# Two-layer retention and RG-LRU decoder step: the order of VectorE and ScalarE in the retention heads, and the PSUM banks of a layer's first k tiles

## The chip, the cores and the metric

One core of one Trainium2 chip runs one program that is launched once. The metric is device time in microseconds from start to end of that program. The kernel before has a median of 2622.69 us over 3 runs.

## The reference

A prompt of 512 tokens and 8 samples of one token each pass through two layers that share their weights. Cut to the part around the change:

```
h = RMSNorm(x)
q, k, v, g_ret, x_lru, y_lru, g_a, g_b = split(h @ w_in)
q = rope(q), k = rope(k) * 256**-0.5          # 4 heads of 256; v has 512 a head
o, S_new = retention(q, k, v, S0)             # S0 = 0 (prompt) or state_ret (samples)
o = groupnorm(o) * gn_gain
ret_branch  = (silu(g_ret) * o) @ w_ret_out
lru_branch  = (gelu(y_lru) * rg_lru(conv(x_lru))) @ w_lru_out
x = x + (sig(g_a) * ret_branch + sig(g_b) * lru_branch) @ w_o
x = x + SwiGLU(RMSNorm(x)); after the last layer a final RMSNorm
```

Retention multiplies a decayed score matrix of q and k with v, adds q times the state of each sample, and updates each sample's state of 256 x 512 numbers (0.5 MB). Everything is float32. The kernel gets that precision from TensorE by splitting each operand into a high part of reduced precision and the low remainder, and by adding three products: high·high, low·high and high·low.

## The kernel before

**Tiles.** The 520 tokens lie along the free axis in two halves of 260; channels lie on the 128 partitions. An output tile of a projection is 128 channels x 520 tokens in two PSUM banks. `whole` computes one from 8 k blocks: 48 matmuls of 128x260. Each layer runs four heads (`one_head`, head 0 written out with `first=True`, heads 1 to 3 in a loop), then the LRU branch, the merge, w_o and the FFN.

**Weights.** They come as a stream of units (1024 columns). SyncE loads a unit, GpSimd (POOL) splits it (L334 high, L337 low in two parts), TensorE (PE) uses it. There are two buffers each, and POOL may start unit u+1 when PE starts unit u.

**A head on PE.** Two q tiles, in heads 1 to 3 the transposes of the last head's output (`turned_back`), two k tiles, in heads 1 to 3 the 8 tiles m0 to m7 of the output projection of the head before (`ret_out`, k dimension 4 blocks, so 24 matmuls each), four v tiles, scores, transposes, gate tile 0, transposes of v (`v_by_token`), gate tiles 1 to 3, then the attention products (`attend`, L576) and the new states (`final_state`, L584). `read_out(b)`, L513, multiplies q by the state of sample b. There are eight of them, placed between and inside the tiles. Each needs the state's high and low part, of which one copy exists. So read-out b, ScalarE's high part of b+1 (`state_high`, L1313) and VectorE's low part of b+1 (`state_low`, L877) follow one another.

**PSUM slots.** q, k, ret_out, v and gate tiles of the heads take turns in two slots `PP`: tile n waits until VectorE has read tile n-2 (`tile_begin`, semaphore t_free, counted in order of the reads). Four further banks `AUX` hold scores, transposes, attention and read-outs. Outside the heads they are half of a ring of four tile slots.

**VectorE (DVE), ScalarE (ACT) and POOL** each run one queue in written order. On DVE `rotate` reads a pair of tiles and forms the rotary result: L845 and L846 read the even tile, L849 and L850 the odd one, L853 and L854 combine them. `read_back` (L765) multiplies the last head's output with the gate and `og_split` (L774) makes its low part, which ret_out m0 waits for. `ret_add` (L780) adds a ret_out tile to `ret_acc`. `gate` (L948) reads a gate tile, `v_low` (L933) and L941 make low parts of v and of the scores, `new_state` (L957) updates a sample's state. ScalarE stores a state after new_state and loads the next one into its place, in the order of its queue.

**A layer's start.** The first two q tiles are made while the norm is still being summed (`twin`). The sums go to AUX banks 0 and 1 (L424), ScalarE takes the root, DVE the reciprocal (L729), scales the cosine and sine tables and then reads the q tiles.

The order inside a head on DVE, before:

```
rotate(0, QF, lambda: None, lambda: None if first else read_back(hh - 1))
...
rotate(KT, KF, new_gain, lambda: None)      # new_gain: og_split(hh), then the new gain
q_parts()                                   # low part of q, q pairs for the read-outs
```

## Time and profile before

| | us |
|---|---|
| median of 3 runs (lowest, highest) | 2622.69 (2619.82, 2623.14) |
| the profiled execution, whole | 2620.91 |
| its span | 2619.1 |
| layer 0: start to end of head 3 | about 0 to 543 |
| layer 0: LRU to FFN | about 543 to 1322 |
| layer 1: heads | about 1322 to 1837 |

A line of the timeline gives start and duration in us, the engine, the source line, the operation with what it writes and reads, and how often it stands there in a row. In brackets stand the idle time of the engine before it and what ended that. Matmuls overlap, so two of them in a row start about 0.24 us after the two before, though each pair shows 0.40. The mean granted TensorE clock of the run is 0.988 of full speed.

### The profile page before, as it was taken

How to read it: one execution, taken by the hardware profiler on the slowest of the kernel's cores; microseconds unless marked ns; L12 is line 12 of the kernel's file. 1: busy time of each engine (PE TensorE's matmuls, PEld its weight loads, DVE VectorE, ACT ScalarE, POOL GpSimd, SP SyncE). 2: the span in 40 equal slices, each digit the busy share in tenths (PEclk: the TensorE clock that was granted, in tenths of full speed). 3: DMA queues.
4: the chain of work that ended last, by engine and by line, in shares of the span. 5: the costliest groups of instructions: out<-in, count | busy, mean ns of one | idle time of the engine just before them, and what ended most of it. 6: DMA issues, size and time to landing. Idle time of an engine off the chain costs nothing.

```text
span 2619.1 us, 52416 instructions
## 1 busy us (share of the span) xinstructions
PE 2495.5 (95%) x19636; PEld 2402.5 (92%) x19636; DVE 1364.9 (52%) x1715; ACT 722.6 (28%) x1109; POOL 1550.7 (59%) x1265
## 2 busy tenths in 40 slices
PE   6999999999999999999989999999999999999997
PEld 6888888899999999999988888888999999999997
DVE  7765656568754542122357656665686546321223
ACT  3423232336731111001123141414367211100111
POOL 4354545457676666666643635353677766666664
PEclk9999999999999999999999999999999999999998
DMA  5545454432233322322246363535222322223222
GB/s 171 186 148 178 149 169 160 158 121 93 75 95 91 97 91 84 94 89 89 89 152 221 106 221 113 204 124 186 85 88 80 98 90 92 89 89 96 88 82 88
DMA packets 121748, 315.69 MB, mean 121 GB/s; under 512 B 12192, under 2 KB 12960, under 8 KB 121568
## 3 DMA queue, kind: packets, MB, share of 16 engines
q1 hardware_dynamic: 60480, 199.78, 24.1%
q10 hardware_dynamic: 61088, 113.34, 12.6%
q8 instruction: 134, 2.20, 0.4%
q14 instruction: 46, 0.38, 0.0%
HBM read 272.69 MB, written 40.38 MB: 120 GB/s over the span
## 4 chain that ended last, share of the span: by engine, by line
PE 68%; DVE 14%; DVEq 6%; issue 4%; ACT 3%; DMA 2%; ACTq 1%; POOL 1%; POOLq 1%; SPq 0%
PE proj L350 40%; PE aux L350 21%; DVE split_scratch L877 2%; PE aux L513 2%; DVE scratch L1044 2%; DVE scratch L957 2%; DMA scratch<-in_sret 1%; DVEq L1189 1%; PE aux L535 1%; PE aux L584 1%; DVE split_scratch L774 1%; POOL w_low L337 1%; POOLq L335 1%; DVE split_scratch L941 1%; PE aux L576 1%
## 5 line engine op out<-in xcount | busy, mean ns | idle before, releaser
L337 POOL TENSOR_TENSOR w_low<-w_raw,w_high 128x512 fp32r<-128x512 f32 (+2 forms) x840 | 1120.3, 1354 | 62.8 <-issue 3.1
L334 POOL TENSOR_SCALAR w_high<-w_raw 128x1024 fp32r<-128x1024 f32 (+3 forms) x420 | 430.0, 1024 | 981.6 <-PE proj L350 770.3
L350 PE MATMUL proj<-x_high,w_high 128*128 128x260 f32 x2816 | 579.8, 287 | 69.1 <-DVE scratch L948 25.2
L350 PE MATMUL proj<-x_low,w_high 128*128 128x260 f32 x2816 | 572.2, 285 | 0.0
L350 PE MATMUL proj<-x_high,w_low 128*128 128x260 f32 x2816 | 572.2, 285 | 0.0
L350 PEld LDWEIGHTS proj<-x_high,w_high 128*128 128x128 f32 x2816 | 442.3, 191 | 83.8 <-DVE scratch L948 27.3
L350 PEld LDWEIGHTS proj<-x_low,w_high 128*128 128x128 f32 x2816 | 439.9, 191 | 0.0
L350 PEld LDWEIGHTS proj<-x_high,w_low 128*128 128x128 f32 x2816 | 439.6, 191 | 0.0
L350 PE MATMUL proj<-split_scratch,w_high 128*128 128x260 f32 x2544 | 414.3, 285 | 16.6 <-DVE ret_acc L780 11.9
L350 PEld LDWEIGHTS proj<-split_scratch,w_high 128*128 128x128 f32 x2544 | 351.7, 189 | 24.3 <-DVE ret_acc L780 13.6
L350 PE MATMUL aux<-x_high,w_high 128*128 128x260 f32 x1280 | 259.1, 283 | 3.2 <-POOL w_low L337 1.7
L350 PE MATMUL aux<-x_high,w_low 128*128 128x260 f32 x1280 | 257.7, 283 | 0.0
L350 PE MATMUL proj<-split_scratch,w_low 128*128 128x260 f32 x1272 | 257.4, 284 | 0.0
L350 PE MATMUL aux<-x_low,w_high 128*128 128x260 f32 x1280 | 257.3, 283 | 0.0
L350 PE MATMUL aux<-split_scratch,w_high 128*128 128x260 f32 x1456 | 235.5, 284 | 0.1
L350 PEld LDWEIGHTS aux<-x_high,w_high 128*128 128x128 f32 x1280 | 197.3, 188 | 5.4 <-POOL w_low L337 3.3
L350 PEld LDWEIGHTS aux<-split_scratch,w_high 128*128 128x128 f32 x1456 | 199.4, 188 | 1.8 <-POOL w_low L337 0.3
L350 PEld LDWEIGHTS proj<-split_scratch,w_low 128*128 128x128 f32 x1272 | 197.5, 190 | 0.0
L350 PEld LDWEIGHTS aux<-x_high,w_low 128*128 128x128 f32 x1280 | 197.2, 188 | 0.0
L350 PEld LDWEIGHTS aux<-x_low,w_high 128*128 128x128 f32 x1280 | 196.8, 188 | 0.0
L877 DVE TENSOR_TENSOR split_scratch<-scratch,split_scratch 128x512 fp32r<-128x512 f32 x128 | 135.3, 1096 | 78.1 <-ACT split_scratch L1313 78.1
L1313 ACT ACTIVATE split_scratch<-scratch 128x512 fp32r<-128x512 f32 x128 | 76.1, 626 | 271.2 <-PE aux L513 271.2
(181 smaller groups left out, 2665.9 us busy)
## 6 DMA issues: line engine op xcount, KB each, us to landing
w_raw<-in_wstream SPq DMA_DIRECT2D x252, 512.0 KB, 3.6
scratch<-in_sret ACTq DMA_DIRECT2D x96, 512.0 KB, 6.4
out_ret_s<-scratch ACTq DMA_DIRECT2D x64, 512.0 KB, 3.5
w_raw<-in_wstream SPq DMA_DIRECT2D x72, 448.0 KB, 3.2
w_raw<-in_wstream SPq DMA_DIRECT2D x48, 384.0 KB, 3.0
scratch<-v_rows ACTq DMA_DIRECT2D x64, 256.0 KB, 4.0
w_raw<-in_wstream SPq DMA_DIRECT2D x48, 320.0 KB, 2.8
out_ret_p<-scratch ACTq DMA_DIRECT2D x8, 512.0 KB, 3.2
```

The lines of the kernel that those rows point to most:

```text
L334: pool.tensor_scalar(WH[:, j, w], WR[:, j, w], 1.0, 0.0, ALU.mult, ALU.add)
L335: pool.drain()
L337: m = pool.tensor_tensor(WL[:, j, part], WR[:, j, part], WH[:, j, part].bitcast(F32), ALU.subtract)
L350: m = pe.matmul(out, wt[:, w, blk * P:(blk + 1) * P], x[xi], start=first and n == 0, stop=last and n == 2)
L513: m = pe.matmul(aux("RO", 2 * NS), QP[:, d, b, :], part[:, d, :], start=b == d == n == 0, stop=b == NS - 1 and d == KT - 1 and n == 1)
L535: m = pe.matmul(aux(f"SC{j}")[:, 0:SEQ - j * P], a[:, d, j * P:(j + 1) * P], b[:, d, j * P:SEQ], start=d == n == 0, stop=d == KT - 1 and n ...
L576: m = pe.matmul(aux(f"AT{t}"), a[:, w], b[:, j, :], start=j == n == 0, stop=j == t and n == 2)
L584: m = pe.matmul(aux(f"ST{d}"), a[:, j, d * P:(d + 1) * P], b[:, j, :], start=j == n == 0, stop=j == TT - 1 and n == 2)
L877: tt(SSL[:, d, :], SS[b % SRING][:, d, :], SSH[:, d, :].bitcast(F32), ALU.subtract).then_inc(s["s_low"], 1)
L957: stt(SS[r], SS[r], KDC[:, TT:TT + 1], TS[u % 2], ALU.mult, ALU.add).then_inc(s["s_new"], 1)
L1044: m = stt(XCF[:, t, d:SEQ], xr[:, 0:SEQ - d], CUR[:, PC_CW + c * CW + j:PC_CW + c * CW + j + 1], XCF[:, t, d:SEQ], ALU.mult, ALU.add)
L1313: A(SSH[:, d, :], SS[b % SRING][:, d, :], copy).then_inc(s["s_high"], 1)
```

## The change

**A layer's first k tiles.** In head 0 they are written to AUX banks: tile 2 to banks 2 and 3, tile 3 to banks 0 and 1, not to the two slots. They wait for the weights alone, tile 3 also for the root of the norm (x_sd), since the norm's sums lie in its banks. The first two v tiles then wait for the reads of q tile 0 and 1, the first read-out for the read of k tile 2.

PE, the end of `twin` in head 0. Before, with the wait for a free slot (t_free):

```order
L350 MATMUL proj<-x_high,w_low 128x260 x2
L367 REGISTER_ALU
L358 REGISTER_ALU [waits w_split]
L350 MATMUL proj<-x_high,w_high 128x260 [waits t_free]
L350 MATMUL proj<-x_high,w_high 128x260
L350 MATMUL proj<-x_low,w_high 128x260 x2
```

Now (proj is the pair of slots, aux the four banks):

```order
L359 MATMUL proj<-x_high,w_low 128x260 x2
L376 REGISTER_ALU
L359 MATMUL aux<-x_high,w_high 128x260 [waits w_split]
L359 MATMUL aux<-x_high,w_high 128x260
L359 MATMUL aux<-x_low,w_high 128x260 x2
L359 MATMUL aux<-x_high,w_low 128x260 x2
```

Between the first k tile and the second one, now:

```order
L359 MATMUL aux<-x_low,w_high 128x260 x2
L359 MATMUL aux<-x_high,w_low 128x260 x2
L516 REGISTER_ALU
L376 REGISTER_ALU [waits x_sd]
L359 MATMUL aux<-x_high,w_high 128x260 [waits w_split]
L359 MATMUL aux<-x_high,w_high 128x260
```

The first k tile goes to aux and t_free is gone from it. The second one waits for x_sd.

**Order of DVE in heads 1 to 3.** q's odd tile, read_back, the combination of q, og_split, and only then the even k tile. After it come q's parts, the gain, state_low(0) and then the odd k tile. ret_add(0) stands between the two combinations of k. The read-outs on PE stand behind m1, m3, m5, m7 and behind each v tile, no longer behind m2, m4, m6 and in the middle of v tiles. ScalarE makes the high part of state 0 ahead of k's.

DVE, heads 1 to 3, from og_split's last two on. Before (p_done: the tile is made, og_high: ScalarE's high part; the even k tile has been read ahead of these rows):

```order
L774 SCALAR_TENSOR_TENSOR split_scratch<-scratch,gn_cur,split_scratch 128x520 [waits og_high] x2
L862 ISA
L862 COPY gn_cur<-params_cur 128x4
L718 REGISTER_ALU
L849 TENSOR_TENSOR scratch<-proj,sin_r 128x520 [waits p_done]
L850 TENSOR_TENSOR scratch<-proj,cos_r 128x520
L853 TENSOR_TENSOR scratch<-scratch 128x520
```

Now (the lines moved by some 20):

```order
L791 SCALAR_TENSOR_TENSOR split_scratch<-scratch,gn_cur,split_scratch 128x520 [waits og_high] x2
L932 ISA
L735 REGISTER_ALU [waits sfin_st]
L866 TENSOR_TENSOR scratch<-proj,cos_r 128x520 [waits p_done]
L867 TENSOR_TENSOR scratch<-proj,sin_r 128x520
L855 ISA
L856 SCALAR_TENSOR_TENSOR split_scratch<-scratch,split_scratch 128x1040 [waits qk_high]
L888 COPY q_pairs<-split_scratch 128x2x8 x2
L935 ISA
L935 COPY gn_cur<-params_cur 128x4
L895 REGISTER_ALU
L896 TENSOR_TENSOR split_scratch<-scratch,split_scratch 128x512 [waits s_high]
```

The split stood between the reads of the two k tiles and stands now ahead of both. Between them stand now L856 (low part of q), L888, L935 and L896 (state_low), and the odd tile's read, L872, follows these.

**Gate 0.** Low parts of the scores come first, then the read of gate tile 0, then all four v_low. ScalarE makes the scores' high parts and issues the loads of the v rows ahead of all four high parts of v.

DVE behind the scores, heads 1 to 3. Before:

```order
L933 TENSOR_TENSOR split_scratch<-aux,split_scratch 128x512 [waits kv_high]
L718 REGISTER_ALU
L948 TENSOR_TENSOR scratch<-proj,rinv 128x520 [waits p_done]
L956 ISA
L957 SCALAR_TENSOR_TENSOR scratch<-scratch,kd_cur 128x1024 [waits t_mul]
```

Now (L987 is the gate's read, L975 v_low):

```order
L982 TENSOR_TENSOR split_scratch<-scratch,split_scratch 128x128 [waits st_high]
L735 REGISTER_ALU
L987 TENSOR_TENSOR scratch<-proj,rinv 128x520 [waits p_done]
L974 REGISTER_ALU
L975 TENSOR_TENSOR split_scratch<-aux,split_scratch 128x512 [waits kv_high]
```

The gate's read stands ahead of the four v_low, no longer behind them.

The diff, cut to its core:

```diff
         def pp(idx):
             return PP[:, slot(idx), :, 0:HALF]
 
+        def key_banks(idx):
+
+            b = 2 * (QK - 1 - idx)
+            return AUX[:, b:b + 2, 0:HALF]
+
+        def first_keys(idx):
+
+            return [key_banks(idx)[:, c, :] for c in range(2)]
...
 
-            def whole(ub, u, tb, idx, hi, lo, midway=None):
+            def whole(ub, u, tb, idx, hi, lo, midway=None, into=None, freed_by=None):
 
 
 
                 unit_begin(ub, u)
-                tile_begin(tb, idx)
-                outs = [PP[:, slot(idx), c, 0:HALF] for c in range(2)]
+                if freed_by is not None:
+                    pe.wait_ge(s["t_free"], freed_by)
+                elif into is None:
+                    tile_begin(tb, idx)
+                outs = into or [PP[:, slot(idx), c, 0:HALF] for c in range(2)]
                 for k in range(MT):
...
                         ub, tb = ub0 - MT // 2 + head * U_HEAD, tb0 - MT + head * T_HEAD
                         uv, v0 = QK + MT // 2, QK + MT
                     if first:
-                        for r in range(RING - 1):
+                        for r in range(RING):
                             pe.wait_ge(r_free[r], layer * USES[r] + 1)
                         tile_begin(tb, 0)
                         tile_begin(tb, 1)
...
                     for i in range(KT, QK):
-                        whole(ub, i, tb, i, XH, XL)
+                        if first and i == QK - 1:
+                            pe.wait_ge(s["x_sd"], layer + 1)
+                        whole(ub, i, tb, i, XH, XL, into=first_keys(i) if first else None)
 
                     def read_out(b):
 
                         if b == 0:
+                            if first:
+                                pe.wait_ge(s["t_free"], tb + (QK - 1))
                             pe.wait_ge(s["qp_full"], hh + 1)
...
                     if first:
                         for i in range(VT):
                             whole(ub, uv + i, tb, v0 + i, XH, XL,
-                                  midway=lambda: read_out(2 * i - 1) if i else None)
+                                  midway=lambda: read_out(2 * i - 1) if i else None,
+                                  freed_by=tb + (i + 1) if i < 2 else None)
                             read_out(2 * i)
                     else:
-                        ret_out(hh, ub, QK, tb, QK, lambda m_: read_out(m_ // 2 - 1) if m_ in (2, 4, 6) else None)
+                        ret_out(hh, ub, QK, tb, QK, lambda m_: read_out(m_ // 2) if m_ % 2 else None)
                         for i in range(VT):
-                            whole(ub, uv + i, tb, v0 + i, XH, XL, midway=lambda: read_out(3 + i))
-                        read_out(NS - 1)
+                            whole(ub, uv + i, tb, v0 + i, XH, XL)
+                            read_out(MT // 2 + i)
                     pe.wait_ge(s["qk_low"], hh * 2 + 2)
 
                     for j in range(TT):
...
+                    def turned(dst, between):
+
                         dve.drain()
                         tt(dst[:, 0, :], dst[:, 0, :], RT[:, 0, :], ALU.subtract)
+                        between()
                         tt(dst[:, 1, :], dst[:, 1, :], RT[:, 1, :], ALU.add).then_inc(s["rope_done"], 1)
                         dve.drain()
...
-                    rotate(0, QF, lambda: None, lambda: None if first else read_back(hh - 1))
-                    dve.wait_ge(s["sfin_st"], hh * 16 + 16)
-                    if first:
-                        state_low(0)
-                    rotate(KT, KF, new_gain, lambda: None)
-                    q_parts()
-                    ts(KSC[:], KF[:, :, SEQ:TOK], DK ** -0.5, None, ALU.mult)
-                    if first:
+                    def key_low():
+
+                        ts(KSC[:], KF[:, :, SEQ:TOK], DK ** -0.5, None, ALU.mult)
                         low(KL, KF, KH, DK ** -0.5, 2)
-                    else:
-                        for m_ in range(MT):
-                            if m_ in (2, 4, 6):
-                                state_low(m_ // 2 - 1)
-                            ret_add(tb, QK, m_)
-                            if m_ == 0:
-                                low(KL, KF, KH, DK ** -0.5, 2)
-                    if not first:
-                        state_low(3)
-                    for e in range(VT):
-                        if e or not first:
-                            state_low(2 * e if first else e + 4)
+
+                    def value(e):
+
                         done(tb, v0 + e)
                         tt(halves(VF[:, e, :]), pp(v0 + e), halves(RINV[:]), ALU.mult
                            ).then_inc(s["t_free"], 1)
-                        if first:
+
+                    turn_even(0, QF)
+                    turn_odd(1)
+                    if first:
+                        dve.wait_ge(s["sfin_st"], hh * 16 + 16)
+                        turn_even(KT, KF)
+                        turned(QF, lambda: None)
+                        turn_odd(KT + 1)
+                        q_parts()
+                        state_low(0)
+                        turned(KF, lambda: None)
+                        dve.tensor_copy(GNC[:], CUR[:, bass.ds(head * VT + PC_GN, VT)])
+                        state_low(1)
+                        value(0)
+                        key_low()
+                        for e in range(1, VT):
+                            state_low(2 * e)
+                            value(e)
                             state_low(2 * e + 1)
+                    else:
+                        read_back(hh - 1)
+                        turned(QF, lambda: None)
+                        og_split(hh)
+                        dve.wait_ge(s["sfin_st"], hh * 16 + 16)
+                        turn_even(KT, KF)
+                        q_parts()
+                        dve.tensor_copy(GNC[:], CUR[:, bass.ds(head * VT + PC_GN, VT)])
+                        state_low(0)
+                        turn_odd(KT + 1)
+                        turned(KF, lambda: ret_add(tb, QK, 0))
+                        ret_add(tb, QK, 1)
+                        key_low()
+                        for m_ in range(2, MT):
+                            if m_ % 2 == 0:
+                                state_low(m_ // 2)
+                            ret_add(tb, QK, m_)
+                        for e in range(VT):
+                            state_low(MT // 2 + e)
+                            value(e)
...
-                    v_low(0)
                     for j in range(TT):
                         dve.wait_ge(s["st_high"], hh * TT + (j + 1))
                         w = slice(ST_OFF[j], ST_OFF[j + 1])
                         tt(STL[:, w], STF[:, w], STH[:, w].bitcast(F32), ALU.subtract
                            ).then_inc(s["st_low"], 1)
-                    for j in range(1, TT):
-                        v_low(j)
...
+                    dve.drain()
                     gate(0)
+                    for j in range(TT):
+                        v_low(j)
                     new_state(0)
...
-                    if first:
-                        state_high(0)
-                    act.wait_ge(s["rope_done"], hh * 2 + 2)
-                    A(KH, KF, copy, scale=DK ** -0.5).then_inc(s["qk_high"], 1)
                     for b in range(NS):
-                        if b or not first:
-                            state_high(b)
+                        state_high(b)
+                        if b == (1 if first else 0):
+                            act.wait_ge(s["rope_done"], hh * 2 + 2)
+                            A(KH, KF, copy, scale=DK ** -0.5).then_inc(s["qk_high"], 1)
...

```

## Rows read from the trace of the kernel before

**Rows 1.** The page, part 1: busy time, share of the span and instructions.
```profile
PE 2495.5 (95%) x19636; PEld 2402.5 (92%) x19636; DVE 1364.9 (52%) x1715; ACT 722.6 (28%) x1109; POOL 1550.7 (59%) x1265
```
**Rows 2.** Waits of PE: line waited for, us in total, times, longest us.
```profile
PE proj L350 <- DVE scratch L948: 25.2, 10, 2.6
...
PE proj L350 <- POOL w_low L337: 12.0, 17, 1.0
PE proj L350 <- DVE ret_acc L780: 11.9, 8, 1.8
PE proj L350 <- DVE scratch L846: 11.5, 2, 5.8
PE aux L513 <- DVE split_scratch L877: 10.0, 22, 0.7
...
PE aux L584 <- ACT scratch L1395: 3.7, 6, 0.8
```
**Rows 3.** Timeline of PE, layer 0, head 0: start, us, instruction, idle before.
```profile
35.64 0.80 PE L350 MATMUL proj<-x_high,w_high 128*128 128x260 f32 x2 [5.75 <-DVE scratch L846]
...
55.66 1.10 PE L513 MATMUL aux<-split_scratch,q_pairs 128*16 128x512 f32 x4 [0.93 <-DVE q_pairs L869]
...
110.06 0.51 PE L350 MATMUL proj<-x_high,w_high 128*128 128x260 f32 x2 [2.15 <-DVE scratch L948]
...
129.24 0.97 PE L584 MATMUL aux<-split_scratch 128*128 128x512 f32 x3 [0.74 <-ACT scratch L1395]
```
**Rows 4.** Chain that ended last: two output tiles (96 products) at three places.
```profile
35.64 13.34 PE proj L350 x96
...
132.95 11.55 PE proj L350 x96
...
507.01 13.22 PE proj L350 x96
```
**Rows 5.** Timeline of DVE, layer 0, head 0.
```profile
29.21 3.40 DVE L729 RECIPROCAL rinv<-rinv 128x520 f32<-128x520 f32 x1 [1.11 <-ACT rinv L1268]
...
34.89 0.69 DVE L846 TENSOR_TENSOR scratch<-proj,sin_r 128x520 f32<-128x520 f32 x1
...
109.30 0.70 DVE L948 TENSOR_TENSOR scratch<-proj,rinv 128x520 f32<-128x520 f32 x1
```
**Rows 6.** Timeline of PE, layer 0, head 1.
```profile
158.50 0.64 PE L350 MATMUL proj<-split_scratch,w_high 128*128 128x260 f32 x4
...
166.28 0.75 PE L350 MATMUL proj<-split_scratch,w_high 128*128 128x260 f32 x4 [1.80 <-DVE ret_acc L780]
...
262.39 3.01 PE L584 MATMUL aux<-split_scratch 128*128 128x512 f32 x12 [0.68 <-ACT scratch L1395]
```
**Rows 7.** Timeline of DVE, layer 0, head 1.
```profile
152.92 0.70 DVE L845 TENSOR_TENSOR scratch<-proj,cos_r 128x520 f32<-128x520 f32 x1 [2.04 <-PE proj L350]
...
154.15 4.95 DVE L774 SCALAR_TENSOR_TENSOR split_scratch<-scratch,gn_cur,split_scratch 128x520 fp32r<-128x520 f32 x4
...
159.97 0.69 DVE L849 TENSOR_TENSOR scratch<-proj,sin_r 128x520 f32<-128x520 f32 x1
...
229.17 0.69 DVE L933 TENSOR_TENSOR split_scratch<-aux,split_scratch 128x512 fp32r<-128x512 f32 x1 [3.98 <-ACT split_scratch L1348]
...
230.07 4.75 DVE L941 TENSOR_TENSOR split_scratch<-scratch,split_scratch 128x512 fp32r<-128x512 f32 x4 [0.21 <-ACT split_scratch L1353]
...
237.43 0.70 DVE L948 TENSOR_TENSOR scratch<-proj,rinv 128x520 f32<-128x520 f32 x1 [0.21 <-issue]
...
256.16 1.28 DVE L957 SCALAR_TENSOR_TENSOR scratch<-scratch,kd_cur 128x1024 f32<-128x1024 f32 x1 [2.55 <-DMA scratch<-in_sret]
```
**Rows 8.** One line each: shortest, median, longest duration in ns, first and last start.
```profile
L877 DVE TENSOR_TENSOR split_scratch<-scratch,split_scratch x128: 678/922/1779, 41.4 to 1776.0; 128x512 fp32r<-128x512 f32 x128
...
L774 DVE SCALAR_TENSOR_TENSOR split_scratch<-scratch,gn_cur,split_scratch x32: 747/1294/1790, 154.1 to 1841.9; 128x520 fp32r<-128x520 f32 x32
...
L839 DVE SCALAR_TENSOR_TENSOR split_scratch<-scratch,split_scratch x16: 1232/1239/2087, 53.0 to 1727.5; 128x1040 fp32r<-128x1040 f32 x16
```

25 lines of the change are left out of this document (10 added, 15 removed).

## The prediction

> **What bounds the kernel now.** I read the busy shares first: PE has 95% of the span, DVE 52% [rows 1]. So the time is PE's work plus its pauses, and a change that moves no matmul can only change pauses and PE's clock. The next view, the waits of PE, shows who ends them [rows 2]. Five of its lines lie in the heads (1.1 us of the second excepted): L948 (a gate tile read late by DVE) 25.2 us, L780 (ret_add) 11.9, L846 (the first q tile of a layer) 11.5, L877 (state_low) 10.0, L1395 (normalisation ahead of the second final_state) 3.7. Together 62.3 us in eight heads, 2.4% of the time. The timeline of PE gives the places, in head 0 [rows 3] and in head 1 [rows 6]. The chain gives the clock: two tiles in a row take 11.55 us at full clock but 13.34 and 13.22 directly after a long pause [rows 4], so a pause can cost up to 1.7 us beyond its own length. The timeline of DVE says how much room its queue has [rows 5, 7].
>
> **A. The first k tiles of a layer (two places).** Before, PE stops 5.75 us [rows 3] between the q tiles and the k tiles, since DVE must first form the reciprocal (from 29.21), scale two tables and read the q tile (until 35.6) [rows 5]. Now both k tiles are made in that time: from 35.64 - 5.75 = 29.9 to 29.9 + 11.55 = 41.4 [rows 3, 4]. The price is at the next stations.
> - The first v tile needs q tile 0's read, 35.6, or up to 2 us later, since POOL now splits weights beside the table products. Wanted at 41.4: hidden.
> - The first read-out, wanted one tile (half of 11.55) later at 47.2, needs q's parts and state_low(0). DVE reads q and k even by 38 to 39 (two operations a tile, 0.61 apart), combines q (two operations at 0.7 to 1.8), reads k odd at 41.6, makes q's low part (1.24 to 2.09 [rows 8]) and state_low(0) (two at 0.68 to 1.78 [rows 8]): ready at 46 to 48.5. So the 0.93 of before [rows 3] goes and 0 to 1.4 comes.
> - The second read-out needs state_low(1), now behind the combination of k: 0.5 to 2 us late. The third has k's low part ahead of it on DVE: 0 to 1.
> I take 2.3 us of new waits (range 0.5 to 4.4). Saved per layer: 5.75 + 0.93 - 2.3 = 4.4, and 1.8 for the slow stretch (13.34 - 11.55 [rows 4]): 6.2. **Two layers: 12.4.** The added wait on the fourth ring entry holds nobody: that bank pair was read before the last one of a layer, which is waited for already. The wait for x_sd is over at 29.2, long before the second k tile.
>
> **B. Gate 0 ahead of v's low parts, heads 1 to 3 (six places).** DVE stood idle 3.98 us until ScalarE had v's first high part, then ran v_low(0), 4.75 us of the scores' low parts and three more v_low, and read the gate tile at 237.43 [rows 7]; PE had waited 2.6 for it [rows 2]. Now the scores' low parts fall into that idle time, and the gate tile is read as soon as it is made. That is before 229.17, since v_low(0) reads transposes that PE made behind it: over 8 us earlier. The wait goes whole, six times 2.6 = 15.6. Behind it v_low and new_state stand earlier: 4.7 less the 1.3 by which v's high parts now stand behind the issue of four loads on ScalarE's queue, so 3.4 to 4.7. State stores and loads follow them on that queue. That matters, since the second final_state (262.39, wait 0.68 [rows 6]) hangs on a state load that lands at 256.16 [rows 7]: with PE 2.6 earlier, it must come 2.6 earlier too. I take that it does (bounds 0 and 4.7) and that 2.2 of the 3.7 us at L1395 [rows 2] go. PE then asks for gate 3 sooner than POOL can split it beside the state updates: 0.3 more at each, -1.8. Slow stretches follow this pause in some heads (13.22 against 11.55 [rows 4]); I count 4 us for six places. **15.6 + 2.2 - 1.8 + 4 = 20.0.**
>
> **B in head 0 (two places).** There two pauses stand at L948, 2.63 and 2.15 (the longest of its line [rows 2], and the second in the timeline [rows 3]). Behind gate 0 DVE runs new_state and the series of lambda, so it reads gate 1 at 109.30 [rows 5]. It is then busy without a gap, and the end of the head is its own: the second final_state at 129.24 waits for it [rows 3]. So PE's gain is what DVE's queue gains, 3.4 to 4.7, I take 4.2. **8.4.** It holds clock and waits.
>
> **C. Heads 1 to 3: og_split and the read-outs (six places).** Removed: 1.80 before m2 [rows 6], six times 10.8, and 10.0 at the read-outs [rows 2]. Read-outs now come behind whole tiles, 6.7 us apart (two ret_out tiles at a quarter of 11.55 each [rows 4], and an estimate of 0.9 for itself: four matmuls of 512 columns against the 24 of 260 in 2.9), while high part, low part and their handovers take about 4. Added: m1 must wait for k's odd tile, which DVE now reads behind og_split and state_low(0). In head 1: the combination of q ends at 152.92 - 2.04 = 150.9 [rows 7]. og_split takes 3.0 (four at 0.75, POOL at rest) to 4.95 [rows 7, 8]: 153.9 to 155.8. k even read: 155.1 to 157.0, ahead of m0 at 158.50 [rows 6], hidden. q's low part 1.24 to 2.09, pairs and gain 0.7 to 1.0, state_low(0) 1.4 to 2.7, k odd read 1.2: 159.6 to 164.0. Before it was 159.97 + 1.2 = 161.2 [rows 7], just in time for m1 at 158.50 + 2.9 = 161.4. So a new wait of 0 to 2.6; with POOL busy about half of that stretch I come to 162.1 and take 0.7. ret_add(0) is done 1.8 later, m2 wants it 3.8 later: gone. **10.8 + 10.0 - 6 x 0.7 + 1 (clock) = 17.6.**
>
> What hides the rest: low parts of k and moved ScalarE work lie beside m2 and the v tiles, with 2 us of room. No transfer changes in size or count.
>
> The Trainium skill speaks against the order in C: "SBUF — State Buffer", Who interferes with whom, says that a VectorE instruction with two SBUF inputs and a GpSimd instruction that reads SBUF exclude each other, the one that comes second waiting for the whole of the other. This trace agrees in size: L774 takes 747 ns at best, 1294 in the median, and L877 678 to 1779 [rows 8]. By the rule at full price all ten such operations between q and k odd would wait; that is rival 1.
>
> **The sum.** 12.4 + 20.0 + 8.4 + 17.6 = 58.4 us. The profiled execution took 2620.9, so 2562.5. The median of the runs shown is 1.8 above it: I predict 2564. With all new waits at zero it is 2552.
>
> **Rivals.**
> 1. *k's odd tile comes late in every head.* Two-input operations on DVE at their long values [rows 8]: read at 163.9 and m1 waits 2.5. 1.8 x 6 = 10.8 more, and the clock's 1 is lost: 2576. For it: og_split took 4.95 in before. Against it: POOL rests 1.2 to 1.5 us between units there.
> 2. *The state loads do not move.* If the transfers around 256.16 are limited by the memory and not by when they are issued, the second final_state stays where it is in six heads: 2.6 and 0.4 are lost in each, 18: 2582. For it: such loads wait 2.55 us for data [rows 7]. Against: the stores ahead of them are issued 4 us sooner, into a time in which PE had stood still.
> 3. *Slower.* The one mechanism is the chain q odd, read_back, combination, og_split, k even, q's low part, state_low, k odd. Each us by which it misses 161.4 costs six. It eats 62.6 (58.4 and the 4.2 counted for it) at 10.4 us of lateness; at 12 us the time is 2622.7 - 62.6 + 72 = 2632. By the longest durations of all (1.79, 2.09, 1.78 [rows 8]) it would be about 6 us late. So nearly excluded.
> 4. *Nothing happens*, since PE's pauses come back one by one at the next station (head 0: read-outs; heads: m1, final_state). A, B and C would have to fail together: 2620.
>
> **How the numbers follow.** Forecast (2552 to 2571) 0.62; rival 1 0.15; rival 2 0.12; both, to 2594, 0.04; better than 2552 0.04; rival 3 0.01; rival 4 0.02. The range reaches to rivals 1 and 2: 2551 to 2586, which leaves out about 0.15. A measurement of this kernel tells 0.2% (5 us) from no change. Faster by more 0.97, within it 0.02, slower 0.01.
>
> **What would show it.** In the waits of PE: L948's line nearly gone in heads 1 to 3 and one of some 0.6 us in each head 0; no pause at the q read of a layer's start, k products on aux directly behind the twin tiles, and small waits for state_low in the first two or three read-outs. A new line of 0.7 us, six times, for the read of k's odd tile (2.5: rival 1); no ret_add wait at m2. The second final_state of head 1 some 3 us nearer to its gate 0, with the state's landing the same amount nearer (if not: rival 2). Wrong would be: q's table products stretched past 41.4, or a wait of several us for w_low, POOL being locked out by DVE.

## The result, and the profile after

| | before | after |
|---|---|---|
| median of 4 runs, same chip (lowest, highest), us | 2622.07 (2619.82, 2623.14) | 2561.57 (2560.41, 2565.22) |
| profiled execution, us | 2620.91 | 2560.41 |
| its span, us | 2619.1 | 2558.6 |
| granted TensorE clock, mean | 0.988 | 0.994 |

The ratio is 0.9773, 95% interval 0.9756 to 0.979. The changed kernel is 60.5 us faster, 2.4 us below the forecast of 2564.0 and inside its range. The interval is about 4.5 us wide on either side, so the medians say nothing on those 2.4 us. The terms of the sum do: one was too high by 6.7 us, and others made up for it. That the total came so close is luck.

Part 1 of the page of after, which answers to [rows 1]. The busy time of PE fell by 17 us with the same 19636 instructions. Part of that is clock: a matmul that runs at the lower of the two levels (1.2 GHz, not 2.4) is longer, and the stretches in which the 128x260 matmuls start further apart than usual cost 22.0 us before and 11.5 after (my sum over the trace). The rest would be overlap that pauses had broken: a read-out split by a pause shows 0.63 + 0.64 us of work (at 303.21 and 304.51 before), an unbroken one 1.09.

```profile
PE 2478.6 (97%) x19636; PEld 2392.2 (93%) x19636; DVE 1342.7 (52%) x1715; ACT 720.9 (28%) x1109; POOL 1553.4 (61%) x1265
```

The waits of PE after: line waited for, us in total, times, longest us. This view answers to [rows 2].

```profile
PE proj L359 <- DVE scratch L873: 13.0, 6, 2.2
PE proj L359 <- POOL w_low L346: 10.4, 16, 1.1
...
PE aux L601 <- ACT scratch L1434: 4.8, 5, 1.4
...
PE proj L359 <- DVE scratch L987: 2.6, 2, 1.5
...
PE aux L529 <- DVE split_scratch L896: 1.3, 2, 0.6
PE aux L593 <- ACT scratch L1434: 1.1, 2, 0.6
PE proj L359 <- DVE ret_acc L797: 1.1, 2, 0.6
```

The gate's wait fell from 25.2 to 2.6 (L987, two left, both in head 0), ret_add's from 11.9 to 1.1, state_low's from 10.0 to 1.3, and the 11.5 of a layer's first q read are gone. **One line is new and large: 13.0 us for the read of k's odd tile (L873), six times 2.16.** The forecast had it at six times 0.7.

The timeline of PE after, in head 0 of layer 0 (above the three dots) and in head 1: start, us, instruction, and in brackets the idle time before it. It answers to [rows 3, 6].

```profile
47.11 1.14 PE L529 MATMUL aux<-split_scratch,q_pairs 128*16 128x512 f32 x4
...
52.24 0.63 PE L529 MATMUL aux<-split_scratch,q_pairs 128*16 128x512 f32 x2 [0.64 <-DVE split_scratch L896]
...
98.33 0.50 PE L359 MATMUL proj<-x_high,w_high 128*128 128x260 f32 x2 [1.04 <-DVE scratch L987]
...
114.45 1.65 PE L593 MATMUL aux<-split_scratch 128*128 128x512 f32 x6 [0.59 <-ACT scratch L1434]
117.54 3.02 PE L601 MATMUL aux<-split_scratch 128*128 128x512 f32 x12 [1.43 <-ACT scratch L1434]
...
152.00 0.74 PE L359 MATMUL proj<-split_scratch,w_high 128*128 128x260 f32 x4 [2.16 <-DVE scratch L873]
156.37 1.24 PE L529 MATMUL aux<-split_scratch,q_pairs 128*16 128x512 f32 x4
...
229.91 0.51 PE L359 MATMUL proj<-x_high,w_high 128*128 128x260 f32 x2 [1.10 <-POOL w_low L346]
...
246.64 2.88 PE L601 MATMUL aux<-split_scratch 128*128 128x512 f32 x12
```

In head 0 the first read-out starts at 47.11 with no wait (55.66 before), and the only wait for a state there is 0.64. In head 1, m1 starts 2.16 us late at 152.00, the read-outs have no wait, and the second final_state (246.64) has none either.

Where the time went can be read from the places at which the heads' scores begin (the first L535 before, L552 after, in us of the PE timeline):

| layer, head | 0, 0 | 0, 1 | 0, 2 | 0, 3 | 1, 0 | 1, 1 | 1, 2 | 1, 3 |
|---|---|---|---|---|---|---|---|---|
| before | 79.46 | 216.73 | 350.68 | 485.55 | 1372.91 | 1510.18 | 1644.14 | 1778.74 |
| after | 71.75 | 204.19 | 331.61 | 461.03 | 1335.73 | 1467.15 | 1594.08 | 1723.10 |
| ahead by | 7.7 | 12.5 | 19.1 | 24.5 | 37.2 | 43.0 | 50.1 | 55.6 |

Split at the last head's end and at m0 as well, the 60.5 us are: A 15.9 (7.9 and 8.0), B in head 0 7.5, B in heads 1 to 3 23.2, C 10.9, and 3 outside the heads. There two stretches at the low clock (granted clock 0.5 at 675 and at 1968 us before) are gone and one is new (at 1280 after), and the waits for w_low are 1.1 us shorter in all. Nothing in the forecast counted these 3 us.

### The profile page after: what moved, and what is told of

Same layout as the page of the kernel before. It is cut to its first block, busy times and chain, and to the rows that moved or that the text cites. A ratio compares the mean times of both kernels' runs of the same rounds, so it can differ in the third digit from the quotient of the medians.

```text
span 2558.6 us, 52418 instructions
## 1 busy us (share of the span) xinstructions
PE 2478.6 (97%) x19636; PEld 2392.2 (93%) x19636; DVE 1342.7 (52%) x1715; ACT 720.9 (28%) x1109; POOL 1553.4 (61%) x1265
## 4 chain that ended last, share of the span: by engine, by line
PE 71%; DVE 9%; DVEq 6%; issue 4%; ACT 3%; DMA 2%; ACTq 2%; POOL 1%; POOLq 1%
PE proj L359 42%; PE aux L359 23%; PE aux L529 2%; DVE scratch L1086 2%; DVEq L1231 1%; PE aux L601 1%; POOL w_low L346 1%; PE aux L552 1%; DMA scratch<-in_sret 1%; DMA scratch<-v_rows 1%; PE aux L593 1%; DVE split_scratch L896 1%; POOLq L344 1%; DVE scratch L1144 1%; ACTq L1578 1%
## 5 line engine op out<-in xcount | busy, mean ns | idle before, releaser
L346 POOL TENSOR_TENSOR w_low<-w_raw,w_high 128x512 fp32r<-128x512 f32 (+2 forms) x840 | 1110.3, 1343 | 62.9 <-issue 3.1
L343 POOL TENSOR_SCALAR w_high<-w_raw 128x1024 fp32r<-128x1024 f32 (+3 forms) x420 | 442.7, 1054 | 918.4 <-PE proj L359 695.3
L359 PE MATMUL proj<-x_high,w_high 128*128 128x260 f32 x2752 | 560.6, 285 | 32.8 <-DVE x_low L743 13.6
L359 PE MATMUL proj<-x_high,w_low 128*128 128x260 f32 x2752 | 555.4, 283 | 0.0
L359 PE MATMUL proj<-x_low,w_high 128*128 128x260 f32 x2752 | 554.9, 283 | 0.0
L359 PEld LDWEIGHTS proj<-x_high,w_high 128*128 128x128 f32 x2752 | 428.1, 189 | 45.2 <-DVE x_low L743 14.0
L359 PEld LDWEIGHTS proj<-x_high,w_low 128*128 128x128 f32 x2752 | 425.3, 189 | 0.0
L359 PEld LDWEIGHTS proj<-x_low,w_high 128*128 128x128 f32 x2752 | 424.9, 189 | 0.0
L359 PEld LDWEIGHTS proj<-split_scratch,w_high 128*128 128x128 f32 x2544 | 352.0, 190 | 25.2 <-DVE scratch L873 14.2
L359 PE MATMUL aux<-x_high,w_high 128*128 128x260 f32 x1344 | 272.0, 283 | 2.6 <-DVE residual L1223 1.4
L359 PE MATMUL aux<-x_high,w_low 128*128 128x260 f32 x1344 | 270.6, 283 | 0.0
L359 PE MATMUL aux<-x_low,w_high 128*128 128x260 f32 x1344 | 270.1, 283 | 0.0
L896 DVE TENSOR_TENSOR split_scratch<-scratch,split_scratch 128x512 fp32r<-128x512 f32 x128 | 141.5, 1146 | 24.7 <-ACT split_scratch L1355 24.7
L359 PE MATMUL aux<-split_scratch,w_low 128*128 128x260 f32 x728 | 146.3, 282 | 0.0
```

Of the source, the lines that this page charges most:

```text
L343: pool.tensor_scalar(WH[:, j, w], WR[:, j, w], 1.0, 0.0, ALU.mult, ALU.add)
L346: m = pool.tensor_tensor(WL[:, j, part], WR[:, j, part], WH[:, j, part].bitcast(F32), ALU.subtract)
L359: m = pe.matmul(out, wt[:, w, blk * P:(blk + 1) * P], x[xi], start=first and n == 0, stop=last and n == 2)
L896: tt(SSL[:, d, :], SS[b % SRING][:, d, :], SSH[:, d, :].bitcast(F32), ALU.subtract).then_inc(s["s_low"], 1)
```

## The experiments

All times are medians. Each run has the kernel before beside it on the same chip, 2620.4 to 2622.7 us. Where two changed kernels that ran on different chips are compared, the difference of their medians is good to a few us only.

### The three parts alone

**a_only** is the kernel before with the banks for the first k tiles and head 0's order on DVE up to the v tiles. **b_only** and **c_only** have the other two parts. Lines from their diffs against before, one place of each (the rest is cut):

```diff
 # a_only, PE, head 0
+                        if first and i == QK - 1:
+                            pe.wait_ge(s["x_sd"], layer + 1)
+                        whole(ub, i, tb, i, XH, XL, into=first_keys(i) if first else None)
 # b_only, DVE behind the scores
-                    v_low(0)
                     for j in range(TT):
...
+                    gate(0)
+                    for j in range(TT):
+                        v_low(j)
 # c_only, PE, heads 1 to 3
-                        ret_out(hh, ub, QK, tb, QK, lambda m_: read_out(m_ // 2 - 1) if m_ in (2, 4, 6) else None)
+                        ret_out(hh, ub, QK, tb, QK, lambda m_: read_out(m_ // 2) if m_ % 2 else None)
```

> Part A alone on the kernel before: a layer's first k tiles in four banks that are free, with the order of head 0 that goes with them; gate 0 and og_split stand as before. The trace of the changed kernel gives 7.9 and 8.0 us for A by the place at which the first scores begin. If the parts add up, PE stays that much ahead to the end of head 0 and the time is 2622 - 16 = 2606 us. The rival: VectorE has no gap at the end of head 0, so A's time stands again there as longer waits (L948 and the second final_state), and A alone gives 8 us or less: 2614 to 2618.

> Part B alone on the kernel before: the scores' low parts ahead of all of v's, gate 0 ahead of v's low parts, and v's high parts behind the issue of the state loads on ScalarE. By the landmarks of the changed kernel it gives 23.2 us in heads 1 to 3 and 7.5 in head 0: 2622 - 31 = 2591 us if the parts add up. The rival: without C, og_split comes late behind the state's last reads and the gain stands again at L780, 1 us in each head: 2597.

> Part C alone on the kernel before: og_split ahead of the first k tile, read-outs behind whole tiles. By the landmarks of the changed kernel it gives 10.9 us net: 20.8 of waits go and 6 x 2.16 us come at the second tile of ret_out. If the parts add up the time is 2622 - 11 = 2611 us and a wait of about 2.2 us for the read of the odd k tile stands in heads 1 to 3. My forecast for C, 17.6, would be 2604 with a wait of 0.7; it would be right if B, which brings PE closer to VectorE there, had made the wait longer.

| | median (lowest, highest) | ratio to before, 95% | against before | expected |
|---|---|---|---|---|
| a_only | 2601.68 (2597.98, 2603.04) | 0.9924 (0.9906 to 0.9942) | -19.9 | -16 |
| b_only | 2589.73 (2586.26, 2591.30) | 0.9878 (0.9860 to 0.9896) | -31.8 | -31 |
| c_only | 2611.76 (2609.03, 2613.17) | 0.9963 (0.9950 to 0.9976) | -9.8 | -11 |

**The parts add up** within what the medians can tell: 19.9 + 31.8 + 9.8 = 61.5, against 60.5 for the whole. The rivals by which one part eats another's gain are out. a_only keeps its lead to the end of head 0: the first final_state starts at 114.46 (122.22 before: 7.8), the second at 121.51 (129.24: 7.7). It gains 4 us more than expected behind the first heads. In its list of waits the gate's are 1.5 us shorter than before (23.7), those for w_low 1.5 and those with no releaser 1.4, and the granted clock is 0.991 against 0.988. Why part A should change these stays open.

C alone has the same new wait as in the whole. The waits of PE in c_only:

```profile
PE proj L359 <- DVE scratch L985: 25.1, 10, 2.6
...
PE proj L359 <- DVE scratch L868: 13.0, 6, 2.2
```

L868 is here the read of k's odd tile. So B, which leaves the gate's 25.1 in place here, has nothing to do with it: the wait belongs to C's own order.

### The cause of the new wait

The timeline of DVE after, head 1, ahead of the odd k tile's read, which answers to [rows 7]. L791 is og_split, L866 k's even tile, L856 q's low part, L888 the pairs, L896 state_low(0), L872 and L873 k's odd tile.

```profile
137.38 1.79 DVE L880 TENSOR_TENSOR scratch<-scratch 128x520 f32<-128x520 f32 x1
139.71 3.98 DVE L791 SCALAR_TENSOR_TENSOR split_scratch<-scratch,gn_cur,split_scratch 128x520 fp32r<-128x520 f32 x4 [0.53 <-ACT split_scratch L1330]
143.61 0.69 DVE L866 TENSOR_TENSOR scratch<-proj,cos_r 128x520 f32<-128x520 f32 x1
...
144.83 2.36 DVE L856 SCALAR_TENSOR_TENSOR split_scratch<-scratch,split_scratch 128x1040 fp32r<-128x1040 f32 x1
147.27 1.12 DVE L888 CAST q_pairs<-split_scratch 128x16 fp32r<-128x16 f32 x2
...
148.37 2.37 DVE L896 TENSOR_TENSOR split_scratch<-scratch,split_scratch 128x512 fp32r<-128x512 f32 x2
150.66 0.69 DVE L872 TENSOR_TENSOR scratch<-proj,sin_r 128x520 f32<-128x520 f32 x1
151.26 0.68 DVE L873 TENSOR_TENSOR scratch<-proj,cos_r 128x520 f32<-128x520 f32 x1
```

The timeline of POOL in the same stretch:

```profile
136.99 3.34 POOL L346 TENSOR_TENSOR w_low<-w_raw,w_high 128x512 fp32r<-128x512 f32 x2
141.72 1.42 POOL L343 TENSOR_SCALAR w_high<-w_raw 128x1024 fp32r<-128x1024 f32 x1 [1.39 <-PE proj L359]
143.29 2.79 POOL L346 TENSOR_TENSOR w_low<-w_raw,w_high 128x512 fp32r<-128x512 f32 x2 [0.15 <-issue]
147.30 1.06 POOL L343 TENSOR_SCALAR w_high<-w_raw 128x1024 fp32r<-128x1024 f32 x1 [1.22 <-PE proj L359]
148.50 3.35 POOL L346 TENSOR_TENSOR w_low<-w_raw,w_high 128x512 fp32r<-128x512 f32 x2
```

Each long operation of DVE lies beside one of POOL: q's low part and state_low(0) beside w_low (L346), the pairs beside w_high (L343). Of og_split's four operations, taken singly, the first took 1.18 us beside w_low and the last 1.53 beside w_high, and the two between them, mostly beside nothing, 0.75. The operations that read PSUM (L866, L872) keep their 0.69 beside a w_low. Two runs take this apart.

**thin_low** makes POOL's w_low short in the heads: it writes 128 columns where the kernel needs up to 512. The other columns hold old values, so its result is not the reference's and only its time is of use. w_high, all matmuls, loads and waits stay.

```diff
+            pool.memset(WL[:].rearrange("p a b -> p (a b)").bitcast(F32), 0.0)
...
+                                q = part if base else slice(part.start, part.start + P)
-                                m = pool.tensor_tensor(WL[:, j, part], WR[:, j, part],
-                                                       WH[:, j, part].bitcast(F32), ALU.subtract)
+                                m = pool.tensor_tensor(WL[:, j, q], WR[:, j, q],
+                                                       WH[:, j, q].bitcast(F32), ALU.subtract)
```

> The changed kernel, but in the 66 weight units that the heads use GpSimd writes w_low for 128 columns of each half of a unit, not for 512; the other columns hold old values, so this part of the result is not the reference's. All matmuls, loads and waits stay. It tells what stretched VectorE's operations ahead of the odd k tile: in head 1 of the changed kernel the odd k tile is read 2.16 us late, behind og_split 3.98, q's low part 2.36 and state_low(0) 2.37 us, each beside a w_low of GpSimd. My theory: those are the weight splits' doing. With them short, the three take about 2.8, 1.3 and 1.3 us (3.3 less), the wait of 2.16 goes in all six places and the time falls by 13 us or more. The rival: they take this long by themselves or beside ScalarE and the transfers; they keep their lengths within 0.5 us, and the wait of 2.16 stays.

Measured: 2534.88 us (2533.34 to 2538.82), ratio to before 0.9665, 95% interval 0.9649 to 0.9681: 26.7 below the changed kernel. The wait for the odd k tile is gone from the list of waits. The same operations on DVE, two lines further down in this kernel's code:

```profile
132.06 0.96 DVE L882 TENSOR_TENSOR scratch<-scratch 128x520 f32<-128x520 f32 x1
133.55 2.77 DVE L793 SCALAR_TENSOR_TENSOR split_scratch<-scratch,gn_cur,split_scratch 128x520 fp32r<-128x520 f32 x4 [0.53 <-ACT split_scratch L1332]
...
137.45 1.23 DVE L858 SCALAR_TENSOR_TENSOR split_scratch<-scratch,split_scratch 128x1040 fp32r<-128x1040 f32 x1
138.78 0.34 DVE L890 CAST q_pairs<-split_scratch 128x16 fp32r<-128x16 f32 x2
...
139.37 1.28 DVE L898 TENSOR_TENSOR split_scratch<-scratch,split_scratch 128x512 fp32r<-128x512 f32 x2
141.67 0.70 DVE L874 TENSOR_TENSOR scratch<-proj,sin_r 128x520 f32<-128x520 f32 x1 [1.01 <-PE proj L361]
```

og_split, q's low part and state_low(0) take 2.77, 1.23 and 1.28 us, where they took 3.98, 2.36 and 2.37: 3.4 less, and DVE now waits 1.01 for PE. **The stretching is POOL's doing.** (w_high keeps its 1.06 us in this kernel, but at 136.39 and 141.97 it lies beside reads of PSUM.) The two profiled executions differ by 24.1 us in span (2558.6 and 2534.5), and 13.0 of that are this wait. In the list of waits the gate's fall by 2.1 more, POOL's own by 2.3, those for the first norm's x_low by 2.3, those for state_low by 1.3 and ret_add's by 1.1, while the normalisation's grow by 4.2 and those with no releaser by 1.5. Of the 8 us that are left, about 5 would be the clock (0.996 against 0.994 of 2535 us, an estimate). The others I can't place.

**k_odd_first** leaves POOL alone and reads the odd k tile earlier.

```diff
                         q_parts()
+                        turn_odd(KT + 1)
                         dve.tensor_copy(GNC[:], CUR[:, bass.ds(head * VT + PC_GN, VT)])
                         state_low(0)
-                        turn_odd(KT + 1)
                         turned(KF, lambda: ret_add(tb, QK, 0))
```

> The changed kernel with one step moved in heads 1 to 3: the odd k tile is read ahead of the gain copy and of state_low(0), not behind them. My theory: the new wait of 2.16 us at the second tile of ret_out is these operations' own time on VectorE (2.4 and 0.3 us), and nothing else needs them that early: the wait goes in all six places, the first read-out (2.9 us later) still finds its state, and the time is 2561.6 - 12 = 2549 to 2552 us. The rival: state_low(0) or ret_add(0) is then late instead, a wait of 1 to 2 us stands at the first read-out or at the third tile of ret_out, and the time stays within 3 us of 2561.6.

Measured: 2547.45 us (2545.28 to 2550.57), ratio to before 0.9717, 95% interval 0.9699 to 0.9734: 14.1 below the changed kernel. The timelines of DVE and (last two rows) PE in its head 1:

```profile
148.65 0.69 DVE L872 TENSOR_TENSOR scratch<-proj,sin_r 128x520 f32<-128x520 f32 x1
149.25 0.68 DVE L873 TENSOR_TENSOR scratch<-proj,cos_r 128x520 f32<-128x520 f32 x1
149.86 0.32 DVE L936 COPY gn_cur<-params_cur 128x4 f32 x1
150.09 2.38 DVE L896 TENSOR_TENSOR split_scratch<-scratch,split_scratch 128x512 fp32r<-128x512 f32 x2
...
150.03 0.70 PE L359 MATMUL proj<-split_scratch,w_high 128*128 128x260 f32 x4
...
152.97 1.09 PE L529 MATMUL aux<-split_scratch,q_pairs 128*16 128x512 f32 x4
```

The odd tile is read by 149.9, m1 starts without a pause, and state_low(0) is done at 152.5, half a microsecond before the first read-out wants it. The pause did not come back elsewhere: the list of waits has none for the odd tile, and the others stay within 1.3 us of what they were. The 14.1 are more than the 13.0 of the pauses and than the 10 to 13 expected, but by less than these medians can tell. (The profiled execution is the slowest of the four and only 9.8 us shorter in span than that of the changed kernel. The slow stretches behind three of the pauses are gone in it, and others, at 638 and 1898 us, have come.) This kernel is faster than the one before and the changed one.

### The two halves of B

**b_scores_only** puts the scores' parts ahead of v's, on both engines, and leaves gate 0 behind v's low parts. **b_gate_only** leaves ScalarE and v_low(0) where they were and puts gate 0 ahead of the other three v_low.

```diff
 # b_scores_only against b_only
-                    dve.drain()
-                    gate(0)
                     for j in range(TT):
                         v_low(j)
+                    gate(0)
 # b_gate_only against b_only (and ScalarE's v_high(0) back ahead of the scores)
+                    v_low(0)
                     for j in range(TT):
                         dve.wait_ge(s["st_high"], hh * TT + (j + 1))
...
                     gate(0)
-                    for j in range(TT):
+                    for j in range(1, TT):
                         v_low(j)
```

> Half of B on the kernel before: the scores' parts ahead of all of v's on VectorE and ScalarE, gate 0 still behind v's low parts. My theory: the idle 3.98 us of VectorE is filled, so gate 0 is read at about 237.4 - 4 = 233.4 in head 1, and TensorE wanted it at 235.4: the wait goes here too, and the state chain behind it moves as in B. So this half gives nearly all of B, 2590 to 2593 us. The rival: the gate must be ahead of v's low parts, since v_low(0) now waits for v's high parts that ScalarE makes behind the loads: a wait of 1 to 2.6 us stays at the gate and the time is 2598 to 2605.

> The other half of B on the kernel before: v's first low part, the scores' parts, gate 0, then v's other three low parts; ScalarE as before. VectorE's idle time of 3.98 us stays, gate 0 comes three operations (2.7 us) earlier, which is as much as TensorE waited: the gate's wait (15.6 us in six places) goes. My theory is that the rest of B (31.8 by its own run) hangs on the state chain, which doesn't start earlier here, while TensorE does: the waits at the second final_state grow and head 0, where VectorE sets the end, gains nothing. 2622 - 15 + 4 = 2608 to 2612 us. The rival: the gate's wait is all that B is about, and this gives 2590 to 2595.

| | median (lowest, highest) | ratio to before, 95% | against before |
|---|---|---|---|
| b_only | 2589.73 (2586.26, 2591.30) | 0.9878 (0.9860 to 0.9896) | -31.8 |
| b_scores_only | 2586.29 (2584.98, 2589.66) | 0.9868 (0.9851 to 0.9884) | -34.1 |
| b_gate_only | 2613.23 (2610.07, 2615.31) | 0.9968 (0.9957 to 0.9980) | -7.1 |

Timeline of PE in b_gate_only, head 0 (first row) and head 1:

```profile
109.33 0.51 PE L359 MATMUL proj<-x_high,w_high 128*128 128x260 f32 x2 [3.67 <-DVE scratch L984]
...
235.08 0.51 PE L359 MATMUL proj<-x_high,w_high 128*128 128x260 f32 x2 [0.16 <-DVE scratch L984]
...
242.18 0.51 PE L359 MATMUL proj<-x_high,w_high 128*128 128x260 f32 x2 [1.08 <-DVE scratch L984]
...
261.34 3.06 PE L596 MATMUL aux<-split_scratch 128*128 128x512 f32 x12 [1.93 <-ACT scratch L1435]
```

Timeline of DVE in b_gate_only, head 1: the idle time ahead of v_low(0), and state update 4.

```profile
228.50 0.69 DVE L972 TENSOR_TENSOR split_scratch<-aux,split_scratch 128x512 fp32r<-128x512 f32 x1 [3.99 <-ACT split_scratch L1388]
...
254.37 1.28 DVE L993 SCALAR_TENSOR_TENSOR scratch<-scratch,kd_cur 128x1024 f32<-128x1024 f32 x1 [3.37 <-DMA scratch<-in_sret]
```

With the gate alone moved, its wait of 2.6 falls to 0.16. But DVE keeps its 3.99 idle us, so all behind is as late as before: 1.08 at the next gate, 1.93 at the second final_state, and in head 0 a longer wait (3.67) for gate 1. In the whole kernel the waits for gates fall from 25.2 to 15.1 us and those for the normalisation grow from 3.7 to 8.2. What paid is that the scores' parts come first. b_scores_only has all of B: no wait for a gate is left in heads 1 to 3 though the gate is read behind the low parts. My forecast had named both moves for the 15.6 us and could not tell them apart. Both times lie outside what I expected: b_scores_only 3.7 us below its range, b_gate_only 1.2 above.

The scores' parts first bring two things at once, and no run parts them. One is the filled idle time. The other was overlooked in the forecast: the four low parts of the scores themselves, two-input operations too, took 4.75 us before, at 230.07 to 234.8 [rows 7], with POOL splitting a unit from 230.35 to 234.7. In the changed kernel they stand where POOL rests (from 213.9 to 217.8) and take 1.70, and it is the same in b_scores_only, while b_gate_only keeps 4.74. The timeline of DVE in the changed kernel:

```profile
213.70 1.70 DVE L982 TENSOR_TENSOR split_scratch<-scratch,split_scratch 128x512 fp32r<-128x512 f32 x4 [1.06 <-ACT split_scratch L1392]
```

The new order also holds on ScalarE, and VectorE's order without ScalarE's was not run.

**gate_behind** asks the same of k_odd_first, where PE is closer behind.

```diff
-                    dve.drain()
-                    gate(0)
                     for j in range(TT):
                         v_low(j)
+                    gate(0)
```

> k_odd_first with one step undone: gate 0 is read behind v's four low parts again, not ahead of them. On the kernel before, the scores' parts ahead of v's gave all of B without this step (2586.3 against 2589.7 us with it). If the step is idle here too, the time is 2547.5 within 3 us, perhaps 2 to 3 lower, and no wait for a gate tile shows in heads 1 to 3. The rival: with A and C TensorE is closer behind, the gate tile is then late by 0.5 to 1 us in six places, and the time is 2551 to 2554 us.

Measured: 2549.20 us (2546.80 to 2552.40), ratio to before 0.9722, 95% interval 0.9706 to 0.9738, against 2547.45 and 0.9717. The ranges overlap, and the only waits for a gate are the two in head 0 (2.4 us in all). The step is idle here too.

### Banks and order in head 0

**banks_old_order** is the changed kernel with DVE and ScalarE of head 0 in the order of before.

```diff
                     if first:
+                        turned(QF, lambda: None)
                         dve.wait_ge(s["sfin_st"], hh * 16 + 16)
+                        state_low(0)
                         turn_even(KT, KF)
-                        turned(QF, lambda: None)
+                        dve.tensor_copy(GNC[:], CUR[:, bass.ds(head * VT + PC_GN, VT)])
                         turn_odd(KT + 1)
+                        turned(KF, lambda: None)
                         q_parts()
-                        state_low(0)
-                        turned(KF, lambda: None)
-                        dve.tensor_copy(GNC[:], CUR[:, bass.ds(head * VT + PC_GN, VT)])
+                        key_low()
+                        value(0)
                         state_low(1)
-                        value(0)
-                        key_low()
...
```

> The changed kernel, but in head 0 VectorE and ScalarE work in the order of before (combination of q, state_low(0), k even, gain, k odd, combination of k, q's low part): of A only the four banks are left. My theory: banks and order are worth something each. The pause of 5.75 us goes by the banks alone, but q's low part now stands behind state_low(0) and both k tiles on VectorE, some 4 to 5 us later than in the changed kernel, so the first read-out waits 3 to 5 us in each layer: 2561.6 + 6 to 10 = 2568 to 2572 us. The rival: the order buys nothing, since VectorE comes level with TensorE during the next v tile: within 3 us of 2561.6.

Measured: 2576.43 us (2569.76 to 2577.15), ratio to before 0.982, 95% interval 0.9804 to 0.9836: 14.9 above the changed kernel (12 by the two ratios), more than the 6 to 10 expected. Timeline of PE in it, the first read-out:

```profile
51.51 1.71 PE L529 MATMUL aux<-split_scratch,q_pairs 128*16 128x512 f32 x4 [3.77 <-DVE q_pairs L888]
```

Timeline of DVE in it: state_low(0) waits for ScalarE, and q's low part comes at 49.69.

```profile
43.17 2.44 DVE L896 TENSOR_TENSOR split_scratch<-scratch,split_scratch 128x512 fp32r<-128x512 f32 x2 [1.66 <-ACT split_scratch L1355]
...
49.69 1.24 DVE L856 SCALAR_TENSOR_TENSOR split_scratch<-scratch,split_scratch 128x1040 fp32r<-128x1040 f32 x1 [0.18 <-issue]
```

The pause of 5.75 is gone by the banks, and 3.77 come back at the read-out. By the start of the first scores (76.82 against 71.75) the order is worth 5.1 us in layer 0: 3.1 of wait (3.77 in place of the 0.64 for state_low) and about 2 for the slow stretch behind it. The rest of the 14.9, some 4 us, lies in heads 1 to 3, where the code is the same. The granted clock is 0.990 against 0.994. Why the slow stretches fall otherwise there stays open.

### The end of head 0

Two runs on top of k_odd_first tried to take the pauses of head 0's end (1.14 for gate 1's read, 0.56 and 1.43 for the normalisation). **terms_late** moves the conv state's terms behind the head and gate 1 ahead of the lambda series. **states_early** also moves the state updates 2 and 3 ahead of the series.

```diff
 # terms_late against k_odd_first
                         series_begin()
-                        for n in (17, 15, 13):
-                            series(n)
                     gate(1)
+                    if first:
+                        for n in (17, 15, 13):
+                            series(n)
...
-                    if first:
-                        state_terms()
                     gate(3)
...
                     invert("AT0")
+                    if first:
+                        state_terms()
 # states_early: gate(1), new_state(2) and new_state(3) all ahead of the series
```

> k_odd_first with two steps moved in head 0 alone: state_terms (2.0 us on VectorE) from ahead of gate 3 to the end of the head, where VectorE has 4.5 us of idle time, and gate 1 ahead of the series' first three terms. In k_odd_first head 0 of the first layer has pauses of 1.14 (gate), 0.56 and 1.43 us (normalisation). If VectorE's queue sets the end of head 0, its gain of 2.0 us is the gain of each layer, and the gate's 1.14 stands again as part of the later wait: 2547.5 - 4 = 2543.5 us. If the pauses are ScalarE's own (state products ahead of the normalisation), the time stays at 2546 to 2548.

> k_odd_first with three steps moved in head 0: state_terms to the end of the head, gate 1 and the state updates 2 and 3 ahead of the whole series of lambda. In terms_late the first two of these moved the pauses, not the time: update 4 waited 1.77 us for a state's load, which ScalarE issues behind updates 2 and 3. My theory now: the end of head 0 hangs on that chain (update 2 and 3, store and load on ScalarE, update 4), so starting it 3 us earlier takes most of the 2.0 to 2.2 us of pauses for the normalisation out of each layer, and the gate's 1.1: 2547.5 - 5 = 2542.5 us. The rival: the load itself or VectorE's queue behind it sets the end and the time stays within 2 us of 2547.5.

Measured: terms_late 2549.32 (2547.67 to 2550.93), states_early 2546.34 (2544.94 to 2547.00), k_odd_first 2547.45 (2545.28 to 2550.57). All three agree within what can be measured; I had expected 2543.5 and 2542.5. Timeline of PE in states_early:

```profile
113.27 1.65 PE L593 MATMUL aux<-split_scratch 128*128 128x512 f32 x6 [0.51 <-ACT scratch L1432]
116.35 3.06 PE L601 MATMUL aux<-split_scratch 128*128 128x512 f32 x12 [1.43 <-ACT scratch L1432]
```

The gate's wait went, and final_state starts at 116.35, not 117.89. But the pauses at the normalisation keep their sum of 1.9 to 2.2 us, whatever VectorE does earlier (1.94 and 0.27 in terms_late). I had expected too much of both: neither DVE's queue (terms_late) nor the state loads (states_early) is all that ends last there. The timeline of ScalarE shows a serial run from the sample tokens' statistics on: loading the table for the root, root, product for update 6, normalisation, product for update 7, root, normalisation. That this is the limit was not tested.

## Why the prediction was right, and where it was not

**What bounds.** Right: PE's work is fixed, and its pauses and clock are the story, with the overlap that a pause breaks. Busy PE went from 95% to 97% of a shorter span.

**A: 12.4 forecast, 15.9 measured, 19.9 alone.** The pause of 5.75, the 0.93 and the slow stretch went as forecast. The mis-sized term is the new waits, 2.3 taken. It was 0.64, one wait for state_low in the middle of the second read-out, at 52.24. 5.75 + 0.93 - 0.64 + 1.8 = 7.8 per layer, which is what was measured. I had taken DVE's durations at the middle of their spread. The read-out found q's parts and state ready.

**B in heads 1 to 3: 20.0 forecast, 23.2 measured.** Right in its main term: L948's wait is gone in all six places. The state chain moved too. Counted from the start of head 1's scores, the update that waited for a load stood at 256.16 - 216.73 = 39.4 us [rows 7], and stands now at 238.73 - 204.19 = 34.5 without waiting (the next one, at 241.19, waits 0.81 for its load). That is 4.9 nearer, against 3.4 to 4.7 forecast. The second final_state is 3.2 nearer (262.39 - 216.73 = 45.7 [rows 6], and 246.64 - 204.19 = 42.4).

Rival 2, loads that do not move, is out: in head 1 ScalarE issues the first of them at 246.35 before and at 229.26 after, and it lands 9.7 and 9.1 us behind its issue.

Two small terms were off and nearly cancel. Of the 2.2 us at the normalisation only 0.3 went: PE came nearer along with the chain, and the waits in these heads are 2.2 in all before and 1.9 after. (With head 0 they grew, from 3.7 to 5.9.) And the feared 0.3 for POOL at each gate 3 (-1.8) did not come: 1.85 before and 1.55 after, in two waits instead of three. What is left of the 23.2, some 6 to 7 us against 4 forecast, is mostly clock and broken overlap: the slow stretches behind this pause (granted clock about 0.5 at 373.5, 507.0 and 1800.2 us before) are gone.

The forecast credited the gate's new place and the filled idle time together. b_gate_only shows that the first without the second gives 7, and b_scores_only that the second without the first gives all, with the 3 us by which the scores' low parts themselves became shorter.

**B in head 0: 8.4 forecast, 7.5 measured.** Right, and for the reason given: PE gains there what DVE's queue gains. The gate's waits went from 2.63 and 2.15 to one of 1.04 (1.54 in layer 1; 0.6 was forecast for each), and the two at the normalisation are now 0.59 and 1.43.

**C: 17.6 forecast, 10.9 measured, 9.8 alone. This is the step that failed.** What it removes is right (10.8 + 10.0 of the waits, to 1.1 and 1.3 in all of the kernel). The failed term is "-6 x 0.7" for the read of k's odd tile: six times 2.16, 8.8 us more.

Rival 1 had this at 2.5 with a chance of 0.15, and its wait is what happened. The total came out at the forecast by luck: A gave 3.5 more, B in heads 1 to 3 3.2 more, and 3 came outside the heads. C itself gave 2.1 more than 17.6 - 8.8, and not by clock, which gave nothing back there (slow stretches behind two pauses before, at 434 and 1729 us, and behind three after). What the forecast left out is that a broken read-out costs more than its listed wait: in head 2 before, one took from 303.21 to 304.99, 1.78 us with 0.68 of wait, and an unbroken one takes 0.93. That is 0.17 for each of the 22, some 3.7 us by this estimate.

Against the forecast's chain, head 1 had 0.53 of waiting for ScalarE ahead of og_split, which was not in it; 2.36 for q's low part, above the longest I had seen (2.09 [rows 8]); and 1.1 for the pairs and the gain (147.27 to 148.37), where I took at most 1.0. With 3.98 for og_split and 2.37 for state_low(0), inside their ranges, the tile was read 5.15 us behind the start of m0 (146.79), not 3.6. "With POOL busy about half of that stretch" was the wrong choice: POOL works one unit per PE tile, and these operations fell on its w_low and w_high.

The Trainium skill's rule in "SBUF — State Buffer", Who interferes with whom, that a VectorE instruction with two SBUF inputs and a GpSimd instruction that reads SBUF shut each other out, named this cause beforehand. thin_low bears it out by 3.98, 2.36 and 2.37 against 2.77, 1.23 and 1.28. I had weighted it too low. At its full price I counted ten such operations between q and k odd. There are nine (two that combine q, four of og_split, q's low part, two of state_low), and in head 1 five of them were stretched, as was one of the two copies of the pairs.

**Rivals 3 and 4** did not occur. The chain missed m1 by 2.16 us, far from the 10.4 at which it would decide. One sum is off: by the listed chances the stated range leaves out 0.11, not 0.15.

## What to carry to other kernels

Fill an engine's idle time ahead of a chain, rather than move the one operation whose wait the profile names: the latter took nearly all of the gate's 2.6 us and gave most of it back at the next stations, the former moved everything behind. When a chain on VectorE decides and GpSimd works beside it, take the durations that its two-input operations have beside GpSimd, not a mean, and look whether they can stand where GpSimd rests (the scores' low parts: 4.75 us or 1.70). And place each read that frees a PSUM slot ahead of work that nobody wants yet: one line moved over a copy and a low part was worth 14 us here.
